# Four small edits to the order of work around a pre-norm projection and a memory norm in a two-block fp32 kernel

## The reference, cut to what matters

```python
mem_n = rms_norm(mem, mem_norm)                       # 256 x 1024
for i in range(2):
    hn = rms_norm(h, norm_pre[i])
    k_m, v_m = (mem_n @ w_mem_kv[i]) split in two
    i == 0: proj = hn @ w_in_a ; latent attention with rotary keys
    i == 1: proj = hn @ w_in_b ; q, k, v, f_logit, q_m, gate = split(proj)
            log_f_cum = cumsum(log_sigmoid(f_logit + b_f))      # the forget rows
    y = concat(attention, memory attention) * silu(gate)
    h = h + rms_norm(y @ w_out[i], norm_post[i])
# second model, layer l: mod = silu(c) @ ada_w[l] + ada_b[l]    # modulation, 12 x 1024 columns in all
```

## Time and profile before

| | us |
|---|---|
| median of 3 runs (lowest, highest) | 2020.9 (2020.48, 2022.31) |
| the profiled execution | 2023.0 |
| its span, first to last instruction | 2021.3 |
| PE busy | 1959.0 |
| DVE, POOL, ACT busy | 1031.0, 784.7, 766.9 |
| mean granted TensorE clock | 0.991 |

### The profile page before, as it was taken

How to read it: one execution, slowest core, us unless ns; L and a number is a source line. 1 busy time by engine, 2 the same in 40 slices (tenths; PEclk the granted TensorE clock), 3 DMA queues, 4 the chain that set the end, 5 groups by cost and what they waited for, 6 DMA issues and landing times.

```text
span 2021.3 us, 23916 instructions
## 1 busy us (share of the span) xinstructions
PE 1959.0 (97%) x9938; PEld 1543.3 (76%) x9938; DVE 1031.0 (51%) x1529; ACT 766.9 (38%) x1171; POOL 784.7 (39%) x347
## 2 busy tenths in 40 slices
PE   7999999999999999999999999999999999999998
PEld 5875666788767698977788888877977877788776
DVE  5325577556776748733566646664911343311323
ACT  5333664422364432165433223324376333312331
POOL 2232553334464452213244334344433433444342
PEclk9999999999999999999999999999999999999999
DMA  7223103356402152121334543453440222233221
GB/s 237 85 58 79 57 1 115 105 169 188 146 1 84 63 179 92 63 63 42 105 125 143 165 150 125 130 157 95 138 131 24 72 84 95 68 105 119 76 74 60
DMA packets 203404, 205.71 MB, mean 102 GB/s; under 512 B 12023, under 2 KB 199675, under 8 KB 203296
## 3 DMA queue, kind: packets, MB, share of 16 engines
q1 hardware_dynamic: 200809, 200.31, 31.2%
q0 software_dynamic: 1472, 3.72, 0.7%
q10 hardware_dynamic: 1015, 0.16, 0.1%
HBM read 201.20 MB, written 2.11 MB: 101 GB/s over the span
## 4 chain that ended last, share of the span: by engine, by line
PE 76%; DVE 8%; POOL 7%; ACT 6%; issue 2%; DMA 1%; ACTq 0%; DVEq 0%; SPq 0%
PE bank L540 43%; PE bank L1125 16%; POOL wl L2341 6%; ACT wh L1336 3%; PE bank L781 2%; PE bank L481 2%; DVE conv L2225 1%; PE bank L805 1%; PE bank L948 1%; DVE conv L2227 1%; PE bank L830 1%; DVE conv L2223 1%; PE bank L1183 1%; PE bank L1193 1%; DVE acc L1777 1%
## 5 line engine op out<-in xcount | busy, mean ns | idle before, releaser
L2341 POOL TENSOR_TENSOR wl<-ring,wh 128x2048 fp32r<-128x2048 f32 (+4 forms) x146 | 620.0, 4247 | 962.0 <-ACT wh L1336 960.3
L1336 ACT ACTIVATE wh<-ring 128x2048 fp32r<-128x2048 f32 (+4 forms) x146 | 256.0, 1754 | 298.1 <-PE bank L1125 129.9
L1777 DVE SCALAR_TENSOR_TENSOR acc<-ring,cs,acc 128x256 f32<-128x256 f32 x336 | 281.3, 837 | 12.0
L540 PE MATMUL bank<-xfh,wh 128*128 128x512 f32 x704 | 277.1, 394 | 7.0 <-POOL wl L2341 7.0
L540 PE MATMUL bank<-xfh,wl 128*128 128x512 f32 x704 | 274.3, 390 | 0.0
L540 PE MATMUL bank<-xfl,wh 128*128 128x512 f32 x704 | 274.0, 389 | 0.0
L540 PEld LDWEIGHTS bank<-xfh,wh 128*128 128x128 f32 x704 | 132.1, 188 | 42.0 <-POOL wl L2341 11.6
L540 PEld LDWEIGHTS bank<-xfh,wl 128*128 128x128 f32 x704 | 132.1, 188 | 27.9
L540 PEld LDWEIGHTS bank<-xfl,wh 128*128 128x128 f32 x704 | 132.2, 188 | 26.5
L1125 PE MATMUL bank<-hsph,wh 128*128 128x512 f32 x352 | 138.8, 394 | 2.3 <-POOL wl L2341 2.3
L1125 PE MATMUL bank<-hsph,wl 128*128 128x512 f32 x352 | 137.7, 391 | 0.0
(11 more groups left out here) (407 smaller groups left out, 4117.1 us busy)
## 6 DMA issues: line engine op xcount, KB each, us to landing
ring<-in_ada_w SPq DMA_DIRECT2D x48, 1024.0 KB, 5.3
ring<-in_ffn_w_in SPq DMA_DIRECT2D x44, 1024.0 KB, 5.1
ring<-in_w_in_b SPq DMA_DIRECT2D x14, 1024.0 KB, 5.3
ring<-in_even_w_in SPq DMA_DIRECT2D x14, 1024.0 KB, 5.1
ring<-in_ffn_w_out SPq DMA_DIRECT2D x16, 768.0 KB, 4.4
ring<-in_odd_w_in SPq DMA_DIRECT2D x12, 1024.0 KB, 6.0
ring<-in_ffn_w_out SPq DMA_DIRECT2D x16, 640.0 KB, 4.1
ring<-in_w_out SPq DMA_DIRECT2D x8, 1024.0 KB, 5.3
```

The source lines that it names most:

```text
L540: mm = eng.matmul(o, l_, r_, start=(first and i == 0), stop=(last and i == 2))
L1336: eng.activation(wh[:, m % SPLIT, h:w], ring[:, n % RING, h:w], ACT.Copy).then_inc(wh_ready, 1)
L1777: ins = eng.scalar_tensor_tensor(out=s, in0=w[:, k, :], scalar=cs[:, k:k + 1], in1=s, op0=ALU.mult, op1=ALU.add)
L2341: eng.tensor_tensor(wl[:, m % SPLIT, h:w], ring[:, n % RING, h:w], wh[:, m % SPLIT, h:w].bitcast(F32), ALU.subtract).then_inc(wl_ready, 1)
```

## The change

It has four parts. (a) In the memory's norm the fillers ahead of the root's spread go from 2 to 3, those behind it from 2 to 7. (b) In `out_first(0)` on ACT, the conversion of the chunk v0 to its high part stands ahead of the second `root()` and not behind it. (c) On DVE one modulation chunk stands between the scaling of the forget rows and the rest of their work, and three, not four, behind it. (d) For the first layer's residual `SHARED` is empty: DVE makes all eight additions, and POOL none; its one call of `low_weights` between them falls away. The second layer's residual stays shared.

```diff
-SHARED = (1, 3, 5)
+SHARED = ((), (1, 3, 5))
...
-            warm(2, n=S // 2)
+            warm(3, n=S // 2)
             norm_spread((mem_normed, KT), 2)
-            warm(2, n=S // 2)
+            warm(7, n=S // 2)
...
                 for t in range(KT):
-                    if t in SHARED:
-                        act.wait_ge(x_shared, l * len(SHARED) + SHARED.index(t) + 1)
+                    if t in SHARED[l]:
+                        act.wait_ge(x_shared, SHARED[l].index(t) + 1)
                     else:
-                        act.wait_ge(x_added, l * (KT - len(SHARED)) + t + 1 - sum(u < t for u in SHARED))
+                        act.wait_ge(x_added, l * KT + t + 1 - sum(u < t for u in SHARED[l]))
...
                     square(x[:, t, :])
+                if l == 0:
+                    split_weights(tile_chunk[index[("in_b.gate", 0)]] + 3)
                 root()
...
-                    if 1 <= t <= KT and t - 1 not in SHARED:
+                    if 1 <= t <= KT and t - 1 not in SHARED[l]:
...
             empty_scaled(("f",), frow[0:HEADS, 0, :], slice(0, HEADS))
+            ada_steps(1)
...
-            ada_steps(4)
+            ada_steps(3)
...
-                for t in SHARED:
+                for t in SHARED[l]:
...
             attention(0)
-            low_weights(tile_chunk[index[("out_a", KT - 1)]] + 2)
-            residual(0)
             low_weights(tile_chunk[index[("out_a", KT - 1)]] + 3)
```

## The result

| us | before | after |
|---|---|---|
| runs side by side on one chip, four of each, median | 2020.69 | 2008.27 |
| their range | 2020.48 to 2022.31 | 2003.43 to 2010.17 |
| profiled execution, time | 2023.0 | 2006.4 |
| its span | 2021.3 | 2003.5 |
| its mean granted clock | 0.991 | 0.998 |

The changed kernel is faster: its time is 0.9933 of that before, with a 95% interval of 0.9913 to 0.9954. On the 2020.9 us from which the forecast started that is 2007.4 us. The sign is right and the gain is larger than I said. The profiled execution gained 17.8 us of span where my sum says 10.5.

A forecast was written before the change was run, and what follows sets the result against it. PE, busy 1959.0 of 2021.3 us, was taken as the bound, so only its pauses and slow stretches could be won. 1.9 + 0.9 + 1.5 + 3.5 + 2.7 = 10.5 us, from 2020.9 to 2010.4, range 2008.2 to 2013.8.

The forecast's parts named there:

- (a) 1.9 us: Memory's norm: more fillers cut PE's pause from 3.44 to 1.2 us, so the 48 products run at 2.4 GHz; 1.9 us.
- The rival of a clock that stays low there: Memory's products: slow clock despite the fillers, gain there only 0.3 us, time 2012.0; 10 in 100.
- (d) 0.9 us: Second block's gate tiles: all residual additions on DVE, PE's 0.84 us wait for the fifth tile goes; 0.9 us.
- (b) 1.5 us: At v0: conversion ahead of the root makes the low part earlier, PE's wait of 1.50 us goes; 1.5 us.
- (c) 3.5 + 2.7 us: At v2: M1 earlier frees its copy; PE's 3.5 us pause goes, and 2.7 us of slow clock behind it.
- The rival of a new wait at v2: At v0 or v2: DVE or POOL held up more than reckoned, PE waits up to 1.5 us, 2012.0; 8 in 100.
- The mild rivals: Slow clock at the memory's products (10 in 100) and a new wait at v0 or v2 (8 in 100), both 2012.0.
- the slower one: From the gate tiles on: low parts every 2.14 us keep PE at 1.2 GHz, up to 2029.4 us; 2 in 100.
- The sum of 10.5 us: Whole kernel: 1.9 + 0.9 + 1.5 + 3.5 + 2.7 = 10.5 us won, median from 2020.9 to 2010.4.
- the last rival: Elsewhere in the program: slow stretches come or go with the shift, 1.7 us each; no chance of its own.

The follow-up runs named there:

- (b) alone: Kernel before with only v0's conversion moved ahead of the root: mean 2020.0 us against 2019.1, ratio 1.0003.
- the second group: Runs on one chip of both kernels unchanged and both with PE delayed by fillers: before 2019.2 us, after 2008.0; delayed, before 2018.6, after 2016.3.
- (c) and (d) alone: Kernel before with only one modulation chunk ahead of the forget rows: 2010.5 us; with only the first residual all on DVE: 2014.7; before 2019.1.
- the 1.9 us delay: Kernel before with two more 512-column fillers on PE ahead of in_b.q, at 465 us: mean 2018.6 us against 2019.2, ratio 0.9997.

## Why the prediction was right, and where it was wrong

**(a) 1.9 us: right, by a reason that doesn't hold.** The pause is 1.28 us, and the products take 10.91 us at 2.4 GHz. The rival of a clock that stays low there is out, in all five executions profiled with the fillers. But I had called 1.2 us the safe side because the nearest rows had kept the clock, and the same trace has the fall behind 1.21 us at 102.28. The length of the pause alone did not assure the term, so that the term came in was in part luck.

**(d) 0.9 us: right.** The rhythm of 2.14 us a tile, the stalls that go with POOL's additions and its low part of f, the one wait that goes: all as worked out. PE's gain grows by 1.0 us at the gate tiles, where I had 0.9.

**(b) 1.5 us: right,** and it needs (c), as the run with (b) alone shows. PE's gain grows by 1.6 us at v0.

**(c) 3.5 + 2.7 us: right,** with 3.5 and 2.5 measured. That M1 would be held up by POOL's low part was the reason for taking 386.5 and not 382.4 as its end; it took 7.85 us for seven instructions that take 3.61 when POOL is silent. The rival of a new wait at v2 came within 1.1 us, and did not happen. The mild rivals and the slower one are all out.

**The sum of 10.5 us: right.** In the profiled pair it is 11.2 up to 660 us, of which 0.5 was there at the start of the program already, from a copy that came sooner: 10.7. With the later pauses filled in both kernels the means differ by 10.7, give or take 1.5.

**The step that failed is the last rival:** "one more or one fewer is half of 3.41 us, 1.7 us ... That is in the forecast's own range." It was wrong in three ways. First, its centre: the execution from which I started had all three later stretches, behind pauses of 1.78, 1.84 and 1.81 us, and a median of 2020.9 which lay 1.6 us over the mean of the kernel's 77 later runs beside others (2019.3). All three runs from which I started were of the upper heap, which is bad luck and no misreading. From there the clock could hardly get worse, only better. Second, its size: the three are worth 2.8, 1.8 and 1.7 us in the profiled pair, 6.3 together where the range allowed 1.7, and the first is 6.83 us long, not 3.41. Third, a reading that stands behind it. I had written that the clock fell only where a pause comes near 3 us. The trace of before held four places that say otherwise (1.21, 1.78, 1.84 and 1.81 us), and I had read the windows at the edits alone. A mean clock of 0.991 over 2021.3 us is 36 us at half speed; the three stretches in my rows are 17 of them (6.83, 3.41 and 6.83), and I did not ask where the rest was.

What the sum gives from the right start: the mean of before in the second group, 2019.2, less 10.5 is 2008.7. The changed kernel's mean there was 2008.0, and the 0.7 us between are within the spread of its runs.

**What stays open.** (c) and (d) alone gained 2.7 and 3.5 us more than their local worth. In both, two of the later stretches were absent in the profiled execution, and the first of them also with the 1.9 us delay; the mean clocks are higher in all three (0.9960, 0.9956 and 0.9947 against 0.9932 to 0.9934). Ten runs of (d) with nine between 2013.1 and 2014.9 are hard to put down to chance. So the shift of the work matters to whether the clock falls behind a pause of 1.8 us; but in what way the runs don't say. They say only that with the pauses filled the effect is gone from these places.

## What to carry to other kernels

Before a change is costed, list every stretch at the lower clock in the whole span, with the pause ahead of each; those behind middling pauses (here 1.2 to 2.9 us) come and go, and where the difference between two profiled executions grows although nothing was changed, look for them first. Compare means over many runs, and read the granted clock of each run beside its time: here 0.001 was about 2 us. Filling these pauses with cheap work in both kernels narrows the runs as well: here it left 10.7 us, give or take 1.5, for a sum of 10.5. Where a chain of waits has two links behind each other, as v0 and v2 here, the first alone is worth nothing until the second is loosened too.

## What the runs showed of the hardware that I had not expected

The same pause was followed by the slower clock in one execution and not in the next. Nine profiled executions have the three later pauses open (both kernels twice, the four parts, the delay of 1.9 us). The one ahead of the second block's sums of squares is 1.78 us in all nine, and the clock fell behind it in four. The one in the scores is 1.83 to 1.85 us, and the clock fell in four, not the same four. The one in the feed-forward's output varies: at 1.81 (twice), 1.88, 1.89, 1.98 and 2.02 us the clock fell, at 1.59, 1.61 and 1.79 it didn't. The 1.20 us ahead of the first block's sums of squares, with the two short pauses behind them, were followed by a fall in seven of the nine. A pause of 1.44 us at 220 us was followed by a fall in one execution. Some longer ones never were: neither the 1.28 us of the memory's norm with the fillers (five executions), nor the 1.36 and 1.54 us at 320 and 930 us (all thirteen profiled executions), nor the 1.50 us at v0 (all eight that have it). So the length of the pause does not tell which ones cost the clock. Even the 2.75 to 2.9 us ahead of the gate tiles were followed by the full clock in four of the nine. Behind the 3.44 or 3.54 us of the memory's norm and the 3.35 to 5.09 us at v2 the clock fell wherever the pause was there.

Apart from the last one, which the end of the program cuts off, a slow stretch is 3.41 or 6.83 us long in the records. It cost 1.7 to 2.8 us of span at the three places, 1.3 at the first block's sums of squares, and nothing in the gate tiles of the kernel before, where DVE's low parts set the pace. These stretches gave the kernel before two heaps of run times, 5 us or 0.25% apart, for identical work.
